# Experts of a two-layer hybrid decoder: outputs and scatters in groups of four experts, slot weights applied to y, top-2 choice by max and max_index

## The reference, cut to what matters

```python
for l in range(2):
    x = mixer_block(x, ...)       # in-projection, three attention-like branches, gates, out-projection
    x = hier_moe_block(x, ...)

def hier_moe_block(x, norm_g, w_rg, b_rg, w_re, b_re, w1, w3, w2):
    xn = rms_norm(x, norm_g)                                   # 256 x 1024
    g_prob = softmax(xn @ w_rg + b_rg)                         # 4 groups
    g_w, g_idx = top_k(g_prob, 1)
    e_logits = (xn @ w_re + b_re).reshape(n_tok, 4, 8)         # 8 experts per group
    e_in = take_along_axis(e_logits, g_idx[:, :, None], axis=1)[:, 0]
    e_w, e_idx = top_k(softmax(e_in), 2)
    e_w = e_w / sum(e_w) * g_w
    combine = zeros(n_tok, 32).at[token, g_idx * 8 + e_idx].add(e_w)
    hid = silu(xn @ w1[e]) * (xn @ w3[e])                      # for each of 32 experts, 256 wide
    return x + sum_e (hid * combine[:, e]) @ w2[e]
```

## Time and profile before

| | |
|---|---|
| median of 3 runs | 1025.53 us (1025.33 to 1029.95) |
| profiled execution | 1027.59 us, span 1025.60 us |
| PE busy | 965.9 us (94%) |
| DVE busy, ACT busy | 479.1 us (47%), 466.2 us (45%) |
| HBM read | 291.05 MB |

### The profile page before, as it was taken

How to read it: one execution, slowest core, us unless ns; L and a number is a source line. 1 busy time by engine, 2 the same in 40 slices (tenths; PEclk the granted TensorE clock), 3 DMA queues, 4 the chain that set the end, 5 groups by cost and what they waited for, 6 DMA issues and landing times.

```text
span 1025.6 us, 19125 instructions
## 1 busy us (share of the span) xinstructions
PE 965.9 (94%) x8018; PEld 784.6 (76%) x8018; DVE 479.1 (47%) x811; ACT 466.2 (45%) x719; POOL 23.7 (2%) x42
## 2 busy tenths in 40 slices
PE   7999999999999999977999999999999899999676
PEld 7898899899886666643598988998998866666344
DVE  6446775567753222211273577654587532222112
ACT  6455555565544333311275464564655443343111
POOL 1010000000000000000000100000000000000000
PEclk9999999999999999988999999999999999999899
DMA  9634544556898999999975246535668799999996
GB/s 301 239 123 164 171 165 164 206 179 233 316 358 313 404 421 419 420 420 420 391 254 177 83 164 187 189 125 205 246 209 358 296 356 408 420 420 420 420 420 255
DMA packets 85478, 293.36 MB, mean 286 GB/s; under 512 B 16976, under 2 KB 17040, under 8 KB 60816
## 3 DMA queue, kind: packets, MB, share of 16 engines
q1 hardware_dynamic: 85392, 292.12, 74.7%
HBM read 291.05 MB, written 1.05 MB: 285 GB/s over the span
## 4 chain that ended last, share of the span: by engine, by line
PE 79%; DMA 11%; DVE 4%; ACT 3%; issue 1%; SPq 1%; POOL 0%; DVEq 0%; ACTq 0%
PE ps_a L775 10%; PE ps_a L777 10%; PE ps_a L776 10%; PE ps_b L1099 8%; DMA units_over_splits<-in_w_dram 8%; PE ps_b L1119 5%; PE ps_a L759 5%; PE ps_b L1178 4%; PE ps_a L761 4%; PE ps_a L760 4%; PE ps_a L1162 4%; DMA units_over_branches<-in_w_dram 3%; PE ps_b L1048 2%; PE ps_b L986 1%; PE ps_b L878 1%
## 5 line engine op out<-in xcount | busy, mean ns | idle before, releaser
L1210 ACT ACTIVATE w_high<-weight_ring 128x1024 fp32r<-128x1024 f32 x166 | 174.8, 1059 | 206.0 <-PE ps_a L777 146.5
L1496 DVE TENSOR_TENSOR w_low<-weight_ring,w_high 128x1024 fp32r<-128x1024 f32 x168 | 202.9, 1225 | 127.2 <-ACT w_high L1210 124.2
L775 PE MATMUL ps_a<-xnT_high,w_high 128*128 128x256 f32 x704 | 201.5, 286 | 1.7 <-DVE xnT_low L1502 1.7
L777 PE MATMUL ps_a<-xnT_high,w_low 128*128 128x256 f32 x704 | 199.5, 283 | 0.0
L776 PE MATMUL ps_a<-xnT_low,w_high 128*128 128x256 f32 x704 | 198.5, 282 | 0.0
L775 PEld LDWEIGHTS ps_a<-xnT_high,w_high 128*128 128x128 f32 x704 | 133.4, 189 | 4.3 <-issue 4.3
L776 PEld LDWEIGHTS ps_a<-xnT_low,w_high 128*128 128x128 f32 x704 | 133.8, 190 | 0.5 <-issue 0.5
L777 PEld LDWEIGHTS ps_a<-xnT_high,w_low 128*128 128x128 f32 x704 | 132.5, 188 | 0.0
L1872 DVE TENSOR_TENSOR y_lo<-ps_b,y_hi 128x512 fp32r<-128x512 f32 x64 | 44.2, 691 | 150.6 <-ACT y_hi L1461 148.6
L1422 ACT ACTIVATE h<-ps_b 128x512 f32<-128x512 f32 x64 | 38.3, 598 | 125.3 <-PE ps_b L1099 125.3
L1178 PEld LDWEIGHTS ps_b<-fold,h 128*128 128x128 f32 x512 | 69.2, 200 | 33.0 <-issue 28.0
(11 more groups left out here) (343 smaller groups left out, 1568.7 us busy)
## 6 DMA issues: line engine op xcount, KB each, us to landing
weight_ring<-in_w_in_dram SPq DMA_DIRECT2D x64, 1024.0 KB, 5.4
units_over_splits<-in_w_dram SPq DMA_DIRECT2D x60, 1024.0 KB, 23.7
units_over_attention<-in_w_dram SPq DMA_DIRECT2D x46, 1024.0 KB, 15.8
weight_ring<-in_w_dram SPq DMA_DIRECT2D x40, 1024.0 KB, 20.7
units_over_branches<-in_w_dram SPq DMA_DIRECT2D x30, 1024.0 KB, 18.6
weight_ring<-in_w_branch_dram SPq DMA_DIRECT2D x12, 1024.0 KB, 5.2
unit_over_gates<-in_w_dram SPq DMA_DIRECT2D x10, 1024.0 KB, 17.9
weight_ring<-in_w_out_dram SPq DMA_DIRECT2D x8, 1024.0 KB, 6.6
```

What stands on the lines that cost most here:

```text
L775: mm(dst, wh, xh, start=row == 0 and s % 2 == 0, stop=False, skip_group_check=True)
L777: last = mm(dst, wl, xh, start=False, stop=row == rows - 1, skip_group_check=True)
L1210: A(mix_buf(whi, i), mix_raw(i), ACT.Copy).then_inc(hi_ready, 1)
L1496: v.tensor_tensor(mix_buf(wlo, i), mix_raw(i), mix_buf(whi, i).bitcast(F32), ALU.subtract).then_inc(lo_ready, 1)
```

## The change

- `GROUPS`: experts go four at a time. `outputs(g)` computes y of four experts into the four strips; the two halves of w2's rows are summed in PSUM (`turn_j`), 16 matmuls. It waits for all four units of w2, and frees them together in its second half. `scatter(g)` is eight matmuls for four experts. Eight of each per layer, 16 before.
- `selectT` has no doubled rows: one PSUM bank and one ACT copy per batch of eight experts instead of two. `select` has no doubled half, and DVE's second `select` of each batch is gone.
- The slot's weight is not multiplied into hid but into y: ACT's copy to `y_hi` has it as scale, DVE's `y_lo` becomes a scalar_tensor_tensor. The weights come as a column: `slot_weights` multiplies `select_weighted` by one column of ones.
- The choice uses DVE's max and max_index (eight largest and their places) on 8 elements per group and tile, 16 instructions in all; those of the first tile stand between the adds to x.
- The order: `hidden(e)`, a gather where e % 8 is 2 to 7, `outputs` of the four before where e % 4 is 0, `scatter` where e % 4 is 1, `hT(e)`.
- 19 ring places and 2 used once (units 9 and 5) instead of 18 and 3 (4, 5 and 9).
- Dummy matmuls: 32 ahead of the last `outputs` in place of 11 ahead of the last but one.

```diff
-    t.act1, t.u = sb("silu_h1", [P, 2, SLOTS]), sb("h3_weighted", [P, 2, SLOTS])
+    t.act1, t.ws = sb("silu_h1", [P, 2, SLOTS]), sb("weight_of_slot", [P, LAST + 1])
...
-    for p in range(PAIRS):
...
+    for e in range(NE):
+        g = GROUP_OF[e]
+        hidden(e)
+        if e == 0:
+            steps.append(("first", 0))
+            selecting.extend((1, piece, 0) for piece in range(2))
+        elif e == 1:
+            steps.append(("first", 1))
+        elif coming and e % BATCH >= 2:
+            gather()
+        if e == 2:
+            steps.append(("first_selT", 0))
+        if e % 4 == 0 and e:
+            outputs(g - 1)
+        elif e % 4 == 1 and e > 4:
+            steps.append(("scatter", GROUP_OF[e - 4]))
+        hidden_T(e)
+        select_next()
+    outputs(LAST)
+    steps.append(("scatter", LAST))
...
-        def outputs(p, n):
-
-            if p == PAIRS - 2:
-                idle_work(11)
-            arrived(pe, n)
-            arrived(pe, n + 1)
-            pe.wait_ge(hid_ready, 2 * p + 2)
-            if p:
-                pe.wait_ge(ylo_done, 2 * p)
+        def outputs(g, n):
+
+            first, count, cuts = GROUPS[g]
+            if g == LAST:
+                idle_work(32)
+            for i in range(count):
+                arrived(pe, n + i)
+            pe.wait_ge(taken, h_used[first + count - 1])
+            if g:
+                pe.wait_ge(ylo_done, 2 * g)
             for n2, done in enumerate((y_first, unit_used)):
...
+                for turn_j in range(2 // cuts):
+                    for c in range(TILES):
+                        e, j = c // cuts, c % cuts + turn_j
                         w2 = unit_buf(n + e)[:, j * D + n2 * 512:j * D + (n2 + 1) * 512]
+                        ins = mm(ps_y[c * SLOTS:(c + 1) * SLOTS, n2, :], t.hid[:, (first + e) % 4, j, :], w2,
+                                 start=turn_j == 0, stop=turn_j == 2 // cuts - 1, skip_group_check=True)
+                        if turn_j == 2 // cuts - 1:
+                            ins.then_inc(done, 1)
...
-                        A(t.yhi[:, n2 * 512:(n2 + 1) * 512], ps_y[:, n2, :], ACT.Copy).then_inc(yhi_done, 1)
+                        A(t.yhi[:, n2 * 512:(n2 + 1) * 512], ps_y[:, n2, :], ACT.Copy,
+                          scale=t.ws[:, g:g + 1]).then_inc(yhi_done, 1)
...
+        def tops(tt):
+            for g in range(NG):
+                last = v.max(t.tops[:, tt, g, :], rest[:, tt, g, :])
+            return ch.mark(last)
+
+        def top_places(tt):
+            for g in range(NG):
+                last = v.max_index(t.top_at[:, tt, g, :], t.tops[:, tt, g, :], rest[:, tt, g, :])
+            return ch.mark(last)
...
+        ch.until(logits_out(0))
+        first_tops = tops(0)
         dve.wait_ge(out_parts, 2)
...
+        in_group = t.in_group[:, :].rearrange("p (g e) -> p g e", g=NG)
+        for i, oh in enumerate((oh1, oh2)):
+            for tt in range(NT):
+                n = ch.mark(v.tensor_tensor(oh[:, tt], in_group, bc(t.top_at[:, tt, :, i], 2, EPG), ALU.is_equal))
...
-        select(0, 0)
+        select(0)
         low(1)
...
-        select(0, 1)
         weigh(0, Chain(dve, again_chain))
```

More of the change, by code:

```diff
@@ L39 @@
 BATCH = 8
-HALF = BATCH // 2
 BATCHES = NE // BATCH
-PAIRS = NE // 2
+GROUPS = [(e, 4, 1) for e in range(0, NE, 4)]
+GROUP_OF = [g for g, (_, count, _) in enumerate(GROUPS) for _ in range(count)]
+LAST = len(GROUPS) - 1
 UNIT = 2048
@@ L64, with steps_of @@
 TOKEN_MAJOR = {"sbv", "mlv", "mbv", "mbq", "mbk", "if"}
-STEPS = [("rows", q) for q in range(NK // 2)] + [("weights", 0)] + [("select", q) for q in range(2)]
+def steps_of(n):
+    groups = [g for g, (e, _, _) in enumerate(GROUPS) if e // BATCH == n]
+    return ([("rows", q) for q in range(NK // 2)] + [("weights", groups)] +
+            [("select", groups[i:i + 2]) for i in range(0, len(groups), 2)])
 def bc(ap, axis, count):
@@ L253, in tensors @@
     sel_at = r.at
[L254 to L256 removed]
+    t.sel, t.selT = sb("select", [P, NT, BATCH, SLOTS], F32R), sb("selectT", [P, 4, SEQ], F32R)
     t.h = sb("h", [P, 2 * FE])
[L258 removed]
+    t.xg = [Region(nc, at, r.at).sb(f"x_grouped_{n}", [P, D]) for n, at in (("first", sel_at), ("second", sel_at + 4 * D))]
+    t.selw = sb("select_weighted", [P, NT, BATCH, SLOTS])
+    t.hid = sb("hid", [P, 4, 2, SLOTS])
     t.ps_a = ctx.enter_context(nc.psum_tensor("ps_a", [P, 4, 512], F32))
@@ L486, in hidden_T, with outputs @@
         h_used.append(banks)
[L488 to L493, removed]
-    def gather():
[L497 to L504, removed]
+    def outputs(g):
+        first, count, _ = GROUPS[g]
+        steps.append(("y", (g, len(order))))
+        order.extend(("w2", e) for e in range(first, first + count))
+        used.extend(count * [used[-1] + TILES])
+        y_used.append(used[-1])
+    selecting, y_used = [], []
+    coming = [(n, i, step) for n in range(1, BATCHES) for i, step in enumerate(steps_of(n))]
+    def gather():
+        nonlocal banks
+        n, i, step = coming.pop(0)
+        steps.append(("gather", (n, *step, banks)))
+        banks += 1
+        if i == len(steps_of(n)) - 1 and n + 1 < BATCHES:
+            selecting.extend((n + 1, piece, banks) for piece in range(2))
     def select_next():
@@ L508, in select_next @@
             steps.append(("selection", selecting.pop(0)))
-    for p in range(PAIRS):
-        last = p == PAIRS - 1
-        hidden(2 * p)
-        if p == 0:
+    for e in range(NE):
+        g = GROUP_OF[e]
+        hidden(e)
+        if e == 0:
             steps.append(("first", 0))
-            selecting.extend((1, piece, 0) for piece in range(3))
-        else:
+            selecting.extend((1, piece, 0) for piece in range(2))
+        elif e == 1:
+            steps.append(("first", 1))
+        elif coming and e % BATCH >= 2:
             gather()
-            if not last:
-                outputs(p - 1)
-        hidden_T(2 * p)
-        if p:
[L522 to L528, removed]
-            steps.append(("first_selT", 0))
[L530 to L536, removed]
+        if e == 2:
+            steps.append(("first_selT", 0))
+        if e % 4 == 0 and e:
[3 more added lines that the diff above has]
+        hidden_T(e)
         select_next()
-    outputs(PAIRS - 1)
-    steps.append(("scatter", PAIRS - 1))
-    assert gathers == (BATCHES - 1) * len(STEPS) and not selecting
+    outputs(LAST)
+    steps.append(("scatter", LAST))
+    assert not coming and not selecting
     ONCE, RING = len(t.once), len(t.ring)
@@ L544, in layer @@
     turn = {n: i for i, n in enumerate(ring_units)}
-    y_used = [used[n] for what, arg in steps if what == "y" for n in arg[1:]]
     def mix_raw(i):
```

226 lines of the change are left out of this document (95 added, 131 removed).

## The result

The changed kernel takes 1038.86 us (median, 1037.47 to 1039.68) where the kernel before takes 1027.47 beside it: a ratio of 1.0104, 95% interval 1.0083 to 1.0125. The profiled execution took 1039.33 us, its span is 1037.4 (1025.6 before). The forecast was 1030.4 with a range of 1021 to 1036, a change of +4.9 us where +11.4 was measured. Of the 8.5 us between 1030.4 and 1038.86, 1.9 are the kernel before, whose median came out at 1027.47 and not at 1025.53; 6.5 are the change, forecast too small. Two of the three terms had the right sign.

What follows compares the result with a forecast made beforehand. The prediction took the experts as bound by DMA at 2.49 us a unit, the last unit's landing and what follows. Start -1.4, tail +2.4 and readiness +3.9 sum to +4.9 us on 1025.5: 1030.4 us, range 1021 to 1036.

Steps and rivals of the forecast that it cites:

- The start of the reloads: Start of each layer's experts: first ring reloads and choice together gain 0.7 us a layer, -1.4 us in two.
- The count of steps: PE's list from 310.2 through the first five experts' hidden and the first y: 24.2 us, four units free at 334.4.
- the hole: DMA dry for 3.1 us, from 332.9 to 336.0, before the first four-unit release; the one at 323 closes.
- the waits of 0.95 us at hT: At hT(2) and hT(3), PE waits for ACT's two copies with nothing ahead to hide it; 0.95 us each.
- The tail: Behind each layer's last unit: 16 matmuls of y instead of eight, 1.2 us net a layer, +2.4 us in two.
- the adds would give half a microsecond back: In the tail: of four adds queued on DVE only the last is still ahead, leaving 1.2 us net.
- Is PE ready: Ahead of the last outputs: low clock and 32 dummies make them 2.8 us late in layer two, 1.1 in one; +3.9.
- That credit: In layer one the two late steps lie 26.54 us apart, 1.7 more than layer two's 24.83, so lateness is 1.1.
- The middle: Some 20 us of PE work a layer taken away, hidden under the DMA's 2.49 us a unit; counted at nothing.
- The choice: Router's expert choice by max and max_index: -0.3 us a layer taken, bounds -0.8 to +0.7.
- Rival (1): Late y: clock low for 8.5 us, 4.2 lost; lateness 5.0 in layer two, 3.3 in one; +10.7, 1036; chance 0.22.
- Rival (3): Start of experts: holes close in both layers, 5.5 of 7.2 us a layer come back; -7.6, 1018; chance 0.10.

Runs made afterwards that it cites:

- after_again: The changed kernel itself, unaltered, timed once more in six runs: 1038.70 us, ratio 1.0095 to the kernel before.
- a_14: The changed kernel with 14 instead of 32 dummy matmuls ahead of each layer's last outputs: 1031.44 us, ratio 1.0033 to the kernel before.
- c_both: Changed kernel with first and last four experts by two, 11 dummies ahead of the last but one outputs instead of the 32: 1024.96 us, ratio 0.9976.
- a_warm: The changed kernel with 30 more dummies ahead of the y of experts 24 to 27: 1033.9 us, ratio 1.0062 to the kernel before.
- b_choice: The kernel before with only the new choice (max and max_index), all else as before: 1025.84 us, ratio 0.9993.
- d_lean: Changed kernel with first and last four experts by two, no dummies ahead of the last two outputs, 5 kept in the last hidden: 1024.03 us, ratio 0.9959.
- e_tail: Changed kernel, last four experts by two, 4 dummies at hT(2) and hT(3), none ahead of the last two outputs: 1024.94 us, ratio 0.9983.

## Why the prediction was wrong

**The start of the reloads (-1.4, measured +0.2).** This term is seen best from the start of the counting (PE's first use of `assigned`) to the last landing of the layer, in us:

| | layer one | layer two |
|---|---|---|
| before | 203.9 | 202.4 |
| after | 206.1, the clock fell | 202.7 |
| after_again | 203.4 | 206.1, the clock fell |
| a_14 | 203.4 | 202.6 |
| c_both | 201.2 | 200.9 |

The count of steps held. From hidden(0) to the first y PE takes 20.9 us in a_14 (309.1 to 330.0), 20.5 as worked out, and the hole stands where it was put. With the clock up the new start is 0.5 us better in layer one and 0.2 to 0.3 worse in layer two; 0.4 better in each is what the forecast leaves without the choice. (a_warm's layer one is an exception, see the end.) What the prediction left out is that the waits of 0.95 us at hT, which the working had put into the list as time only, cost clock as well. One such fall delays the first four units by 3.3 us and the last landing by 2.7 to 3.3 us in its layer, and turns the gain into a loss. The failed step is the one that puts 0.95 at hT(2) and hT(3) and counts full speed behind them. Ahead of the counting each layer is 1.3 and 1.1 us shorter, some 0.9 of it by the choice; the rest differs by run, as the second mixer does, which with the same instructions takes 290.5 us in some profiles and 292.0 in others, from its first matmul to the counting. The section "A second HAM failure mode: psum-queue depth-cycling" of the Trainium skill's page TensorE: Matmul & The Clock Gate says that short idle times of PE between groups of matmuls, if they are frequent enough, make the clock go down and up again; these traces agree, at gaps of 1.02 us, in some runs and not in others.

**The tail (+2.4, measured 3.8).** The second copy starts 1.74 us later, as worked out (1.72). Wrong was that the adds would give half a microsecond back: DVE walks its list in order, the four adds stand behind the second y_lo, and all four (2.47 us) are still ahead when it ends, as they were in the kernel before. The whole 1.7 reaches the end; in layer one it is 2.1. That the scale on the copy is free was nearly right: 0.69 for 0.60, 0.75 for 0.69.

**Is PE ready (+3.9, measured 6.8).** The mechanism, the place and the order were right: the idle time was 9.0 us, the clock fell in both layers, the dummies ended late and the last y stood behind them. Two sizes were off. The low clock reached 5.0 and 5.2 us into y, not 4.0, and cost 2.4 to 2.5 us, not 2.0: 0.9 in two layers. And in layer one the prediction had credited the last unit with 1.7 us more time, from the earlier trace rows; after the change it had 24.7 us from y to landing and not 26.54. That credit was not a property of the layer but of one trace: there the last unit took 4.2 us (504.0 to 508.2). After the change it took 2.7, and in b_choice, which has the same order of loads as before, 2.9. What slowed it in that trace stays open. Taking a distance of one trace for a constant was the failed step; the 24.83 of layer two was the right one for both. These two are 2.7 of the 2.9 us that were missing.

**The middle** cost nothing, as forecast: 421 GB/s from 345 to 430 us, 420 before. **The choice** starts the counting at 303.00, 0.9 us earlier (the router is 0.4 earlier in this run, which is not counted), just outside its bound of -0.8; what it brings in the median can't be told apart from nothing.

**The rivals.** Rival (1)'s 1036 was nearest in number, but by too dear a clock: 4.2 us a layer where 2.5 were measured. Its condition, a low stretch that reaches past y and hT(28), was not met: y was back at full clock before its end. It had the same credit in layer one and the same short tail, and no loss at the start. Rival (3), the holes closing, is what c_both does (393 GB/s), but it needs twos at the start, and from the counting to the last landing it brings 2.6 and 1.4 us a layer and not 5.5. (It is rival (1), not the second, whose cost the prediction calls that of the clock rule applied to every wait.)

## What to carry over

When PE has just been given less work it stands longer, and its clock pays for it: where the work taken away was hidden, ask at each new wait what runs behind it, and whether that leads to the end. Collecting four units instead of two is harmless in the middle of a stream and costs at both its ends; two at the ends and four between beat both kernels (d_lean takes 0.4% less than the kernel before and some 1.4% less than the changed one). Dummies in an in-order queue must end ahead of the arrival that they bridge also when the work in front of them ran at half clock: 32 cost some 7 us against 14, and none at all cost some 2.5 against 14.

## What the runs showed of the hardware

The granted clock fell to 0.50 some 1.2 us after a wait of PE of 1.02 us, with PE otherwise busy, and again after the second such wait. Whether it did was a matter of the run: the changed kernel shows it in layer one in one profile and in layer two in another. The spread of a kernel's runs is no sign of it: the kernel before, in whose profile these steps keep the clock, spreads by 5.5 to 6.2 us in sets of 17 to 35 runs, and e_tail by 8.7.

After a wait of 7.7 to 9.4 us the y of experts 24 to 27, 3.64 us at full clock, took 4.9 to 6.6 us in both layers of every profile of the changed kernel and of its variants without the 30 dummies.

MAX8 on 8 elements takes some 0.09 us (four in 0.37), and a max_index, which is the pair MATCH_VALUE_LOAD and FIND_INDEX8, starts every 0.14, in DVE's timeline of the changed kernel:

```profile
296.67 0.37 DVE L1727 MAX8 top_logits<-logits 128x8 f32<-128x8 f32 x4
...
299.37 0.08 DVE L1733 MATCH_VALUE_LOAD top_places<-top_logits,logits 128x8 f32 x1
299.44 0.16 DVE L1733 FIND_INDEX8 top_places<-top_logits,logits 128x8 uint32<-128x8 f32 x1
299.52 0.07 DVE L1733 MATCH_VALUE_LOAD top_places<-top_logits,logits 128x8 f32 x1
```

Open is what sets the 2 us by which some variants' starts differ with the clock up in both (the last landing of a_warm's layer one is 4.5 us behind that of a_14, of which 2.0 are a later start of the counting).
